# Attention stage: products of the exponentials with v in fp32 on two column tiles, steps taken in pairs

## The reference

```python
s = jnp.einsum('bqhd,bkhd->bhqk', q, k).astype(jnp.float32) * ATTN_SCALE
s = s + qc[query] - kc[key]          # cumulative log forget gates
s = jnp.where(causal, s, NEG_INF)
p = jax.nn.softmax(s, axis=-1)
att = jnp.einsum('bhqk,bkhd->bqhd', p.astype(v.dtype), v)
```

## Time and profile before

| | us |
|---|---|
| median of 3 runs | 3212.57 (3211.2 to 3220.07) |
| profiled execution, its own time | 3211.89 |
| its span, first to last instruction | 3210.2 |
| PE, DVE, ACT, POOL busy in the span | 3031.9, 2071.8, 1612.0, 811.6 |
| attention stage, PE's first to last matmul | 485.6 to 976.2 |

### The profile page before, as it was taken

The page is one execution under the profiler, slowest core; times in us unless marked ns, Lnnn a source line. Parts: engine busy times, 40 slices in busy tenths (PEclk is TensorE's granted clock), DMA queues, the critical chain, the costliest instruction groups (busy, mean ns, idle before and its releaser), DMA issues. The chain is left out here.

```text
span 3210.2 us, 57421 instructions
## 1 busy us (share of the span) xinstructions
PE 3031.9 (94%) x19548; PEld 2415.4 (75%) x19548; DVE 2071.8 (65%) x4223; ACT 1612.0 (50%) x3155; POOL 811.6 (25%) x1437
## 2 busy tenths in 40 slices
PE   8999968999999989999999999999999999999677
PEld 8999956787777867777777777777777777777433
DVE  5333437787786547766778666786666776664465
ACT  3111115676673114566446665456664456664255
POOL 1110010000001114344444343543444544423000
PEclk9999988998999989999999999999999999999889
DMA  5443454224204447677887677887777867756284
GB/s 209 130 134 109 128 151 119 67 54 93 74 1 141 138 159 263 204 245 251 287 272 272 218 247 252 301 257 244 245 242 272 297 227 246 245 177 246 86 344 179
DMA packets 270570, 628.11 MB, mean 196 GB/s; under 512 B 52343, under 2 KB 116759, under 8 KB 262303
## 3 DMA queue, kind: packets, MB, share of 16 engines
q1 hardware_dynamic: 169719, 306.89, 30.0%
q0 software_dynamic: 93760, 296.83, 26.9%
q10 hardware_dynamic: 6800, 20.71, 1.9%
HBM read 557.09 MB, written 67.33 MB: 195 GB/s over the span
## 5 line engine op out<-in xcount | busy, mean ns | idle before, releaser
L1519 PE MATMUL F_ps_u<-X_x_hi,F_w_hi 128*128 128x512 f32 x1408 | 578.2, 411 | 10.8 <-DVE F_w_lo L1749 10.8
L1520 PE MATMUL F_ps_u<-X_x_lo,F_w_hi 128*128 128x512 f32 x1408 | 561.1, 399 | 0.0
L1521 PE MATMUL F_ps_u<-X_x_hi,F_w_lo 128*128 128x512 f32 x1408 | 560.7, 398 | 0.0
L1749 DVE TENSOR_TENSOR F_w_lo<-X_raw,F_w_hi 128x512 fp32r<-128x512 f32 x352 | 239.2, 681 | 271.5 <-ACT F_w_hi L1656 269.8
L1959 POOL DMA_DIRECT2D F_kin<-cache_k x512 | 278.8, 545 | 311.9 <-issue 190.1
L1999 POOL DMA_DIRECT2D F_vin<-cache_v x512 | 282.8, 552 | 284.1 <-issue 163.5
L1519 PEld LDWEIGHTS F_ps_u<-X_x_hi,F_w_hi 128*128 128x128 f32 x1408 | 267.2, 190 | 103.6 <-issue 34.9
L1656 ACT CAST F_w_hi<-X_raw 128x512 fp32r<-128x512 f32 x352 | 214.3, 609 | 255.1 <-PE F_ps_y L1521 230.8
L1521 PEld LDWEIGHTS F_ps_u<-X_x_hi,F_w_lo 128*128 128x128 f32 x1408 | 267.0, 190 | 64.8
L1806 DVE STREAM_TRANSPOSE F_kt<-F_kin 128x1024 f32<-128x1024 f32 x256 | 303.5, 1222 | 14.9 <-DMA F_kin<-cache_k 14.6
L1520 PEld LDWEIGHTS F_ps_u<-X_x_lo,F_w_hi 128*128 128x128 f32 x1408 | 267.6, 190 | 56.9
(11 more groups left out here) (327 smaller groups left out, 6723.0 us busy)
## 6 DMA issues: line engine op xcount, KB each, us to landing
F_kin<-cache_k POOLq DMA_DIRECT2D x512, 256.0 KB, 3.5
F_vin<-cache_v POOLq DMA_DIRECT2D x512, 256.0 KB, 4.4
X_raw<-w_up_t SPq DMA_DIRECT2D x120, 512.0 KB, 5.2
F_raw<-w_up_t SPq DMA_DIRECT2D x56, 512.0 KB, 5.0
X_raw<-w_down SPq DMA_DIRECT2D x56, 512.0 KB, 4.9
S_raw<-w_up_t SPq DMA_DIRECT2D x22, 1024.0 KB, 12.5
sc_qk<-A_early SPq DMA_DIRECT2D x16, 1024.0 KB, 5.1
F_forget<-sc_wT POOLq DMA_DIRECT2D x256, 64.0 KB, 3.0
```

Source lines behind the costliest of these rows:

```text
L1519: nc.tensor.matmul(out, a_hi, b_hi, start=first, stop=False)
L1520: nc.tensor.matmul(out, a_hi, b_lo, start=False, stop=False)
L1521: return nc.tensor.matmul(out, a_lo, b_hi, start=False, stop=last)
L1749: nc.vector.tensor_tensor(w_lo[:, q % 4, :], raw[q // 2 % RAW][:, q % 2 * 512:(q % 2 + 1) * 512], w_hi[:, q % 4, :].bitcast(F32), ALU.subt ...
```

## The change

POOL copies v once as fp32; `sc["v"]` has 64 columns per head and not 128. In the attention stage a step's exponentials are copied from PSUM once, as fp32, into one of eight buffers `p`: of even steps by DVE, of odd steps by ACT, each with its own semaphore for the bank (`t_free[0]`, `t_free[1]`; `free_of` says for every use of a bank who releases it). The product with v is one fp32 product of 64 weight columns: for even key blocks into rows 0 to 63 of `ps_o`, for odd ones into rows 64 to 127 (`side`), in groups with g = 0 all into rows 0 to 63. The loops go by pairs of steps: transposes of both, the logits that both steps would issue, both products with v of the pair before, then a group's turning back (NAT_AFTER, now in pairs).

```diff
-        vcat = early[:, 2048:3072].rearrange("p (h a d) -> p h a d", h=H, a=2)
+        v_kept = early[:, 2048:2048 + AW].rearrange("p (h d) -> p h d", h=H)
...
-                sp.dma_start(sc["v"][:, :, t, :].rearrange("h p c -> p h c"),
-                             vcat[:, :, :, :].rearrange("p h a d -> p h (a d)")).then_inc(v_stored, 16)
+                sp.dma_start(sc["v"][:, :, t, :].rearrange("h p c -> p h c"), v_kept).then_inc(v_stored, 16)
...
-                nc.gpsimd.tensor_copy(vcat[:, :, 0, :].bitcast(F32R), v).then_inc(v_hi_done, 1)
-                pool.wait_ge(v_hi_done, t + 1)
-                nc.gpsimd.tensor_tensor(vcat[:, :, 1, :].bitcast(F32R), v, vcat[:, :, 0, :], ALU.subtract).then_inc(v_cat, 1)
+                nc.gpsimd.tensor_copy(v_kept, v).then_inc(v_cat, 1)
...
-    PBUF = 4
-    LAG = 3
-    NAT_AFTER = 5
+    PBUF = 8
+    PAIRS, NAT_AFTER = NTR // 2, 2
...
+    def sides(n):
+        return 2 if groups[n][1] else 1
...
-                    pe.wait_ge(t_free, tk - TBANKS + 1)
+                    owner, count = free_of[tk - TBANKS]
+                    pe.wait_ge(t_free[owner], count)
...
             def times_v(i):
                 n, k = turns[i]
                 h, o = groups[n][0], skip(i) * P
-                pe.wait_ge(t_free, tick_of[i] + 1)
+                side = k % sides(n)
+                owner, count = free_of[tick_of[i]]
+                pe.wait_ge(t_free[owner], count)
...
-                nc.tensor.matmul(ps_o[:, o:512], v[:, h % 2, k, :], p_hi[:, i % PBUF, o:512], start=k == 0, stop=False,
-                                 skip_group_check=True)
-                nc.tensor.matmul(ps_o[:, o:512], v[:, h % 2, k, :], p_lo[:, i % PBUF, o:512], start=False,
-                                 stop=k == steps[n] - 1, skip_group_check=True).then_inc(pv_done, 1)
+                nc.tensor.matmul(ps_o[side * HD:(side + 1) * HD, o:512], v[:, h % 2, k, :], p[:, i % PBUF, o:512],
+                                 start=k < sides(n), stop=k >= steps[n] - sides(n), skip_group_check=True).then_inc(pv_done, 1)
...
-            for i in range(NTR + LAG + 2):
-                if i < NTR:
+            for pair in range(PAIRS + 2):
+                i = 2 * pair
+                if pair < PAIRS:
                     transposes(i)
-                    for n, r, j in logits_at.get(i, []):
+                    transposes(i + 1)
+                    for n, r, j in logits_at.get(i, []) + logits_at.get(i + 1, []):
                         logits(n, r, j)
-                if LAG <= i < NTR + LAG:
-                    times_v(i - LAG)
-                for n in nat_at.get(i, []):
+                if 1 <= pair <= PAIRS:
+                    times_v(i - 2)
+                    times_v(i - 1)
+                for n in nat_at.get(pair, []):
                     turn_back(n)
...
-                nc.vector.tensor_tensor(p_lo[:, i % PBUF, o:512], ps_t[:, tick_of[i] % TBANKS, o:512],
-                                        p_hi[:, i % PBUF, o:512].bitcast(F32), ALU.subtract).then_inc(t_free, 1)
+                nc.vector.tensor_copy(p[:, i % PBUF, o:512], ps_t[:, tick_of[i] % TBANKS, o:512]).then_inc(t_free[0], 1)
...
-                nc.scalar.copy(p_hi[:, i % PBUF, o:512], ps_t[:, tick_of[i] % TBANKS, o:512]).then_inc(hi_done, 1)
+                nc.scalar.copy(p[:, i % PBUF, o:512], ps_t[:, tick_of[i] % TBANKS, o:512]).then_inc(t_free[1], 1)
...
-SCRATCH = {"qk": (4, AC, P, SEQ), "v": (H, P, TILES, P), "wfold": (G, P, D), "q_s": (S, AW), "aug": (H, 4, SEQ), 
+SCRATCH = {"qk": (4, AC, P, SEQ), "v": (H, P, TILES, HD), "wfold": (G, P, D), "q_s": (S, AW), "aug": (H, 4, SEQ), 
```

More of the change, by code:

```diff
@@ L807, in stage_attention @@
     for n in range(NGR):
-        nat_at.setdefault(min(first_t[n + 1] - 1 + NAT_AFTER, NTR + LAG + 1), []).append(n)
+        nat_at.setdefault(min(first_t[n + 1] // 2 - 1 + NAT_AFTER, PAIRS + 1), []).append(n)
     tick_of, nat_tick = {}, {}
     tick = 0
-    for i in range(NTR + LAG + 2):
-        if i < NTR:
-            tick_of[i] = tick
-            tick += 1
-        for n in nat_at.get(i, []):
+    for pair in range(PAIRS + 2):
+        if pair < PAIRS:
+            for i in (2 * pair, 2 * pair + 1):
+                tick_of[i] = tick
+                tick += 1
+        for n in nat_at.get(pair, []):
             nat_tick[n] = tick
             tick += 1
+    free_of, frees = {}, [0, 0]
+    odd_ticks = {tick_of[i] for i in range(1, NTR, 2)}
+    for t in range(tick):
+        owner = int(t in odd_ticks)
+        frees[owner] += 1
+        free_of[t] = (owner, frees[owner])
+    def sides(n):
+        return 2 if groups[n][1] else 1
     def skip(i):
@@ L914, in turn_back @@
                 pe.wait_ge(o_copied, n + 1)
-                pe.wait_ge(t_free, tk - TBANKS + 1)
+                owner, count = free_of[tk - TBANKS]
+                pe.wait_ge(t_free[owner], count)
+                deep = HD * sides(n)
                 for r in range(4):
-                    last = nc.tensor.matmul(ps_t[:, tk % TBANKS, r * HD:(r + 1) * HD], oT[:, n % 2, r * P:(r + 1) * P], both[:, :],
-                                            start=True, stop=True)
+                    last = nc.tensor.matmul(ps_t[:, tk % TBANKS, r * HD:(r + 1) * HD], oT[0:deep, n % 2, r * P:(r + 1) * P],
+                                            both[0:deep, :], start=True, stop=True)
                 last.then_inc(nat_done, 1)
@@ L948, in copy_logits, with copy_p @@
                         .then_inc(least_ready, 1)
-            def rest(i):
+            def copy_p(i):
                 o = skip(i) * P
-                dve.wait_ge(hi_done, i + 1)
+                dve.wait_ge(t_done, i + 1)
                 if i >= PBUF:
                     dve.wait_ge(pv_done, i - PBUF + 1)
-                nc.vector.tensor_tensor(p_lo[:, i % PBUF, o:512], ps_t[:, tick_of[i] % TBANKS, o:512],
-                                        p_hi[:, i % PBUF, o:512].bitcast(F32), ALU.subtract).then_inc(t_free, 1)
+                nc.vector.tensor_copy(p[:, i % PBUF, o:512], ps_t[:, tick_of[i] % TBANKS, o:512]).then_inc(t_free[0], 1)
             def normalise(n):
@@ L969, in normalise @@
                                         ps_t[:, nat_tick[n] % TBANKS, 0:4 * HD].rearrange("p (r d) -> p r d", r=4),
-                                        rec[:, n % 4, :].unsqueeze(2).to_broadcast([P, 4, HD]), ALU.mult).then_inc(t_free, 1)
+                                        rec[:, n % 4, :].unsqueeze(2).to_broadcast([P, 4, HD]), ALU.mult).then_inc(t_free[0], 1)
             for r, j in parts_of(0):
                 copy_logits(0, r, j)
[L974 to L977, removed]
+            for pair in range(PAIRS + 3):
+                i = 2 * pair
+                if 1 <= pair <= PAIRS:
+                    copy_p(i - 2)
+                for n in nat_at.get(pair - 1, []):
                     normalise(n)
-                for n, r, j in logits_at.get(i, []):
+                for n, r, j in logits_at.get(i, []) + logits_at.get(i + 1, []):
                     copy_logits(n, r, j)
@@ L994, in exp, with copy_p @@
                                      accum_out=total[:, n % 4, r, j:j + 1]).then_inc(exp_done, 1)
-            def high(i):
+            def copy_p(i):
                 o = skip(i) * P
@@ L1006, in o_out @@
                     act.wait_ge(nat_done, n - 1)
-                nc.scalar.copy(oT[:, n % 2, :], ps_o[:, :]).then_inc(o_copied, 1)
+                nc.scalar.copy(oT[0:HD * sides(n), n % 2, :], ps_o[0:HD * sides(n), :]).then_inc(o_copied, 1)
             for r in range(4):
@@ L1011, in _ @@
                     exp(0, r, j)
[L1012 to L1019, removed]
+            for pair in range(PAIRS + 1):
+                i = 2 * pair
+                if pair < PAIRS:
+                    copy_p(i + 1)
+                if pair and i == first_t[turns[i - 1][0] + 1]:
+                    o_out(turns[i - 1][0])
+                for n, r, j in exps_at.get(i, []) + exps_at.get(i + 1, []):
                     exp(n, r, j)
```

11 lines of the change are left out of this document (6 added, 5 removed).

## The result

The changed kernel takes 3222.52 us (median of 8 runs, 3219.03 to 3225.6) beside 3213.81 us for the kernel before on the same chip (8 runs): a ratio of 1.0026, 95% interval 1.0015 to 1.0037. It is slower, as forecast, but by 9 us where +38 stood; the range's lower end of 3210 holds it. The runs do tell these 0.26% from none, which the prediction doubted for anything under 0.3%.

The account below looks back on a forecast made before the run. PE was taken to bound the projection and, with DVE and ACT near full, the attention stage. Terms 41 + 2 - 7 + 2 = +38 us on 3211.89 gave 3250 us, range 3210 to 3295.

Parts of the forecast that it names:

- The clock: Attention stage: a tenth runs at 1.2 GHz, so added work costs 2 us more; bounds 24 back, 10 lost.
- the switch: On PE, per pair of steps: entering tiles +0.15, leaving +0.09, first transposes afterwards +0.10; together +0.34 us.
- the +41: PE's added us in attention groups with g of 1 to 3: 25.0 for full pairs, 15.8 for group ends.
- The full pair: Products with v of two full steps on PE: 0.86 us where they cost 0.94, so -0.08.
- The g = 0 groups: Attention groups on one tile: 12 us more work, but PE waits there anyway; counted 2, bounds 0 and 12.
- The stalls: At attention group starts, PE's 39.4 us of waits for exponentials fall by 7; bounds 0 and 39.
- The overlap of the tiles: Products with v: passes of the even and odd block run side by side, two at a time, 0.43 us each.
- the rival in which they run one behind the other: Products with v: the two tiles do not overlap at all, 3354 us; tiles not overlapping had chance 0.07.
- The rival "faster": Attention stage: exponentials are done when PE arrives and the clock stays up; about 3192 us, chance 0.16.
- The rival "it cancels out": Attention stage: two thirds of the possible gain from waits and clock comes back; 3212 us within 0.3%, chance 0.08.
- The projection: POOL's subtraction of 23.6 us goes, v's store and load carry half the bytes; PE covers all: 0.
- the waits that moved: Attention: PE's waits for DVE's and ACT's copies stay covered by its other work: no cost; uncovered output copies 18 us.

Follow-up runs that it names:

- The first experiment: Kernel before, filled with 12 or 20 idle transposes in PE's pauses where two g = 0 groups meet: 3196.72 us beside 3215.11, ratio 0.9946.
- experiment 3: Changed kernel with the products of two pairs (four steps) run together, one entry into the tiles and one exit per four steps: 3249.16 us, ratio 1.0106.
- experiment 2: Kernel before with only the loops by pairs of steps, both fp32r products, conversions and subtractions kept: 3207.05 us beside 3215.11, ratio 0.9973.
- The sixth experiment: Changed kernel with every product with v in one column tile: 3322.44 us in one run.
- experiments 4 and 7: 4: changed kernel with 8 idle transposes at the meetings, 3228.34 us; 7: kernel before with pairs of steps and 12 or 20 idle transposes, 3203.31 us.
- experiment 11: Kernel before with 6 and 10 idle transposes in PE's pauses where two g = 0 groups meet: 3203.20 us, ratio 0.9964.
- experiment 5: Changed kernel with the g = 0 groups, all but the first, on two tiles too: 3221.32 us, ratio 1.0028.

## Why the prediction was right in direction and wrong in size

- **The step that failed is "The clock".** It said: a tenth of the stage runs at 1.2 GHz, so the added work costs 2 us more there, with 24 back only "if no stall were left". By the weight loads the stalls did not go (33 shorter ones took the place of 28 with long ones), yet the clock stayed up; PE's own idle time for the exponentials fell from 27.7 us to 6.7. The first experiment prices this term by itself at 13.1 us of gain; I had entered a loss of 2. That is 15 of the 26 us between +38 and the +12.3 of the two profiles. I had read the pauses of the earlier trace rows only as room in which longer products cost nothing, and not asked what PE's work in that room does to the clock of the group behind it.
- **The second is a mis-sized term, the switch.** By the changed kernel's distances it is 0.29 us, by experiment 3's falling g = 1 groups 0.285 (its longer groups gave less), and not 0.34: entering costs 0.14 (0.09 and 0.05 in the first round) for 0.15, leaving 0.10 for 0.09, the transposes behind tiles 0.05 for 0.10. That last one is the term which no row showed. With 0.29, 144 pairs cost 144 x 0.05 = 7 us less: the +41 should have been some +34. The full pair itself (0.86 against 0.94) was right.
- **The g = 0 groups**, taken at +2: against the filled kernel the second ones of a meeting are 1.08 us shorter each, the first ones 0.17 longer, the very last 0.75 longer; about -2 in all. Longer products cost nothing there, as said; that the pairing shortens the way to the next exponentials (experiment 2) was not foreseen.
- **The stalls**, taken at -7: 32.1 us are left for the exponentials (32 forecast). 34 - 2 - 7 = 25, and 25.4 is measured over the filled kernel. The agreement of the sum is better than that of its terms, and in part luck: the weight loads' waits for the copies, taken at no cost, rose from 7.1 us to 26.8 (13.4 of products and 6.9 of transposes for DVE's, 6.5 of transposes for ACT's), and how much of that PE felt is not shown.
- **The overlap of the tiles**: as forecast. The sixth experiment gives 0.85 us a pair and 3322 us for the kernel; the rival in which they run one behind the other had 3354.
- **The rival "faster"** had the right mechanism (the clock stays up with PE's pauses gone or short) and a wrong reason for it (that ACT is done earlier): pairing and longer products on PE cover the wait. It needed more than 43 of its 63 us; some 20 came, 13 of clock and 7 of waits.
- **The rival "it cancels out"** (3212 within 0.3%, with a chance of 0.08) is the nearest to what was measured, +9 us or 0.26%, though that is clear of none. The direction came out right by a quarter of the margin that was forecast.
- **The projection and the waits that moved**, taken at 0: the stage begins 2.4 us later in the profile of after, within what such profiles differ by (485.5 to 488.5 in this study). PE itself shows no idle time for the odd copy (eight weight loads wait 0.8 us each for it), and only 0.3 us for the output copy; ahead of the products stand 7.4 us of idleness, for DVE's copy (first of the groups above).

The Trainium skill, "TensorE: Matmul & The Clock Gate", Part 3 (Packing small matmuls), has matmuls start and end strictly in program order. With the two passes of a product next to each other, as the prediction took it, the trace does not agree for fp32 products in different tiles: in strict order the four passes would need three rounds, and they take two (1.01 us against 1.86 in one tile).

## What to carry to other kernels

An idle stretch of TensorE can have a second price, the clock of the work that follows; price it from the granted clock of the next stretch, not from the wait. Before a change is credited or blamed, put idle work into the pauses of the kernel before: that gives the base with the clock up, here worth 18 us (13 of them seen in the stage) and more than the whole change. Size the filler to the pause: where the pauses were shorter (experiments 4 and 7) it cost time itself. Count the changes between full array and tiles like instructions, 0.2 to 0.3 us each here, and remember that bunching work to save them can lay bare the next group's chain (experiment 3).

## What the runs showed of the hardware that was not expected

- The same pauses did not always have the same effect. The clock fell to 1.2 GHz after PE stood idle for 0.73 and 1.39 us with two products between at two meetings of the kernel before (at 611.8 and 734.7) but not at the third; after 0.74 and 2.00 us at two of three meetings in experiment 11; after 0.90 and 1.14 us at one of three in experiment 5. It did not fall at any meeting of the changed kernel, with 0.68 and 0.82.
- Idle transposes of the identity were enough to hold the clock at 2.4 GHz, and in experiment 1, where they lay within the pauses, the groups outside the meetings kept their times within 0.1 us.
- Two tiles' fp32 passes run so closely side by side that a pair of products of 512 columns costs 1.01 us, entry round and exit included, and in one tile 1.86.
